# Gate tiles of block 2 in 512-wide products

## The reference

```
h = rms_norm(x, g_attn)
proj = h @ w_in                      # q, k, v of two attentions, and gates: 2 x 1024 columns
o_diff = differential attention, 4 heads
o_sb   = stick-breaking attention, 8 heads
g_diff, g_sb = split(sigmoid(gates + b_gate))
merged = g_diff * (o_diff @ w_o_diff) + g_sb * (o_sb @ w_o_sb)
x = x + merged @ w_out
x = x + (silu(h2 @ w_gate) * (h2 @ w_up)) @ w_down,   h2 = rms_norm(x, g_ffn)
```

## Time and profile before

| | |
|---|---|
| median of three runs | 1475.91 us |
| profiled execution | 1474.18 us, span 1472.4 us |
| busy TensorE, its weight loads, VectorE, ScalarE | 1351.3, 1104.7, 785.6, 593.5 us |
| chain that ended last | TensorE 71%, DMA 22%, VectorE 3% |
| mean granted clock of TensorE | 0.965 of full speed |

### The profile page before, as it was taken

One profiled execution on the slowest core, in us unless ns is written; L12 is line 12 of the kernel. 1 busy time (PEld: TensorE's weight loads), 2 busy tenths in 40 slices (PEclk: granted clock), 3 DMA queues, 4 the chain that ended last, 5 costly groups with the idle time before them and its releaser, 6 DMA issues.

```text
span 1472.4 us, 22657 instructions
## 1 busy us (share of the span) xinstructions
PE 1351.3 (92%) x9775; PEld 1104.7 (75%) x9775; DVE 785.6 (53%) x1168; ACT 593.5 (40%) x811; POOL 14.7 (1%) x32
## 2 busy tenths in 40 slices
PE   8999999997776777767899999999999999999998
PEld 7898998753343334333689999888999999988886
DVE  6656677411111011100678877877567786877753
ACT  5554654210100010101536664655433576455542
POOL 0000000000000000000010000000001000000000
PEclk9999999999899798988999999999999999999999
DMA  9553458899999999999764435656536434566640
GB/s 315 190 177 115 170 202 336 358 426 427 426 426 427 427 427 426 427 427 423 282 192 165 172 132 190 195 172 229 200 115 201 172 121 166 172 200 189 225 172 29
DMA packets 117404, 377.08 MB, mean 256 GB/s; under 512 B 8215, under 2 KB 53623, under 8 KB 104759
## 3 DMA queue, kind: packets, MB, share of 16 engines
q1 hardware_dynamic: 115879, 371.52, 66.0%
q0 software_dynamic: 1424, 4.08, 1.0%
HBM read 372.42 MB, written 1.06 MB: 254 GB/s over the span
## 4 chain that ended last, share of the span: by engine, by line
PE 71%; DMA 22%; DVE 3%; issue 1%; ACT 1%; SPq 1%; POOL 0%; ACTq 0%; DVEq 0%
PE bank L658 21%; PE bank L668 10%; DMA SZ<-in_w_exp_up 8%; DMA ring<-in_w_exp_up 6%; PE bank L670 5%; PE bank L947 5%; PE bank L1321 4%; PE bank L1315 4%; PE bank L1122 3%; PE bank L721 3%; PE bank L691 3%; DMA SZ<-in_w_exp_down 3%; DMA tail_hn<-in_w_exp_up 3%; PE bank L1152 2%; PE bank L1075 2%
## 5 line engine op out<-in xcount | busy, mean ns | idle before, releaser
L1909 DVE TENSOR_TENSOR parts<-ring,parts 128x2048 fp32r<-128x2048 f32 x155 | 351.3, 2288 | 79.0 <-ACT parts L1422 76.2
L1422 ACT ACTIVATE parts<-ring 128x2048 fp32r<-128x2048 f32 x152 | 284.9, 1908 | 95.0 <-PE bank L1321 27.4
L658 PE MATMUL bank<-SKr,parts 128*128 128x256 f32 x1824 | 226.5, 284 | 2.2 <-DVE parts L1909 2.2
L658 PEld LDWEIGHTS bank<-SKr,parts 128*128 128x128 f32 x1824 | 220.8, 192 | 3.9 <-DVE parts L1909 1.9
L668 PE MATMUL bank<-hnr,parts 128*128 128x512 f32 x640 | 222.5, 393 | 0.0
L670 PE MATMUL bank<-hnr,parts 128*128 128x256 f32 x640 | 177.9, 278 | 0.0
L668 PEld LDWEIGHTS bank<-hnr,parts 128*128 128x128 f32 x640 | 119.9, 187 | 27.3
L1122 PE MATMUL bank<-ring,TMP 128*32 128x512 f32 x576 | 85.3, 745 | 49.7 <-DMA ring<-in_w_exp_up 49.7
L2303 DVE COPY KV<-bank 128x256 f32<-128x256 f32 x16 | 6.8, 425 | 222.2 <-PE bank L1102 222.2
L670 PEld LDWEIGHTS bank<-hnr,parts 128*128 128x128 f32 x640 | 120.4, 188 | 0.1
L658 PE MATMUL bank<-hnr,parts 128*128 128x256 f32 x864 | 107.8, 285 | 0.0
(11 more groups left out here) (393 smaller groups left out, 2058.9 us busy)
## 6 DMA issues: line engine op xcount, KB each, us to landing
ring<-in_w_in SPq DMA_DIRECT2D x60, 1024.0 KB, 7.3
ring<-in_w_ffn_in SPq DMA_DIRECT2D x44, 1024.0 KB, 7.1
ring<-in_w_exp_gate SPq DMA_DIRECT2D x18, 2048.0 KB, 39.3
ring<-in_w_exp_up SPq DMA_DIRECT2D x18, 2048.0 KB, 43.9
ring<-in_w_exp_down SPq DMA_DIRECT2D x18, 2048.0 KB, 38.8
ring<-in_w_ffn_out SPq DMA_DIRECT2D x20, 1024.0 KB, 6.6
G<-in_w_exp_gate SPq DMA_DIRECT2D x7, 2048.0 KB, 39.1
SZ<-in_w_exp_up SPq DMA_DIRECT2D x7, 2048.0 KB, 43.9
```

The costliest lines, as they stand in the source:

```text
L658: m = mm(b(name)[:, T * half:T * half + T], part(chunk, ws)[:, k, P * mt:P * mt + P], src[xs][:, k, :], start=k == 0 and i == 0, stop=k == ...
L1422: A(parts[:, 2 * (r % 2), 2048 * i:2048 * i + 2048], ring[:, CHUNK[chunk][0], 2048 * i:2048 * i + 2048], ACT.Copy).then_inc(high_made, 1)
L1909: v.tensor_tensor(parts[:, 2 * (r % 2) + 1, at], ring[:, CHUNK[chunk][0], at], parts[:, 2 * (r % 2), at].bitcast(F32), ALU.subtract).then_ ...
```

## The change

The twelve tiles of the head loop are made by `wide_tile`, each in a bank of its own (ga2a, ga2b and so on: twelve names per layer instead of six). Both parts of the input lie side by side in `SKr`, the low part first, so the lower half of a bank gets Whi xlo + Wlo xhi and the upper half Whi xhi. For each tile ScalarE copies the upper half into the tile's place in `hx`, VectorE adds the lower half to it, and when both tiles of a pair are there VectorE multiplies the pair in place by the normalisation factor. The sigmoids wait for these multiplications by a count. In the head loop ScalarE's copies of turn h-1 stand behind the weights of head h+1, and VectorE's additions where the multiplications stood.

```diff
-            s += [name for name, half in GATE_HALVES[h] if half == 0]
+            s += [f"{name}{'ab'[half]}" for name, half in GATE_HALVES[h]]
...
-                 ("ga0", "ga1"), ("ga1", "ga3"), ("gb0", "gb1"), ("gb1", "gb3"), ("proj_diff", "pa3"),
+                 ("ga0", "ga1"), ("ga1", "ga3b"), ("gb0", "gb1b"), ("gb1", "gb3b"), ("proj_diff", "pa3"),
...
-            def wide_tile(chunk, name, mt):
+            def wide_tile(chunk, name, mt, src=hnr, high=0):
...
-                    mm(b(name)[:, :].rearrange("p (s n) -> p s n", s=2), part(chunk, 0)[:, k, P * mt:P * mt + P], hnr[:, :, k, :],
+                    mm(b(name)[:, :].rearrange("p (s n) -> p s n", s=2), part(chunk, 0)[:, k, P * mt:P * mt + P], src[:, :, k, :],
                        start=k == 0, stop=k == KT - 1, skip_group_check=True)
-                    m = mm(b(name)[:, 0:T], part(chunk, 1)[:, k, P * mt:P * mt + P], hnr[:, 0, k, :],
+                    m = mm(b(name)[:, 0:T], part(chunk, 1)[:, k, P * mt:P * mt + P], src[:, high, k, :],
                            start=False, stop=k == KT - 1, skip_group_check=True)
...
                     for name, half in GATE_HALVES[h]:
                         j = int(name[2])
-                        split_tile(f"{name[:2]}{j // 2}{x}", z_parts, name + x, 2 * (j % 2) + half)
+                        wide_tile(f"{name[:2]}{j // 2}{x}", f"{name}{'ab'[half]}{x}", 2 * (j % 2) + half,
+                                  SKr[:, 0:4096].rearrange("p (s k n) -> p s k n", s=2, k=KT), 1)
...
-                def gate_sigmoid(name, z, row):
-
-                    emptied(act, name)
+                def gate_sigmoid(pairs, z, row):
+
+                    act.wait_ge(gate_scaled, 6 * l + pairs)
...
+                def gate_lows_of(h):
+
+                    for name, half in GATE_HALVES[h]:
+                        full(act, f"{name}{'ab'[half]}{x}")
+                        A((ga if name[1] == "a" else gb)[:, 2 * int(name[2]) + half, :], b(f"{name}{'ab'[half]}{x}")[:, T:2 * T],
+                          ACT.Copy).then_inc(gate_low_out, 1)
+
                 for h in range(8):
...
                     if h < 7:
                         sb_weights(h + 1)
+                    if h:
+                        gate_lows_of(h - 1)
                     if h in (0, 2, 4):
                         sb_softplus(h + 2)
...
                 act.preload_act_table(ACT.Sigmoid)
-                gate_sigmoid("ga3" + x, ga, 0)
+                gate_lows_of(7)
+                gate_sigmoid(2, ga, 0)
                 second_highs("bo3" + x, 3)
                 high("proj_sb" + x)
-                gate_sigmoid("gb3" + x, gb, 8)
+                gate_sigmoid(6, gb, 8)
...
                     for name, half in GATE_HALVES[h]:
+                        z, j, bank = ga if name[1] == "a" else gb, int(name[2]), f"{name}{'ab'[half]}{x}"
+                        dve.wait_ge(gate_low_out, 12 * l + sum(len(g) for g in GATE_HALVES[:h]) + GATE_HALVES[h].index((name, half)) + 1)
+                        freed(v.tensor_tensor(z[:, 2 * j + half, :], b(bank)[:, 0:T], z[:, 2 * j + half, :], ALU.add), bank)
                         if half:
-                            take_scaled(name + x, two(ga if name[1] == "a" else gb, int(name[2])), by_attn)
+                            emptied(dve, f"{name}a{x}")
+                            emptied(dve, bank)
+                            v.tensor_tensor(two(z, j), two(z, j), by_attn, ALU.mult).then_inc(gate_scaled, 1)
```

More of the change, by code:

```diff
@@ L377, in build @@
         hid_silu, hid_scaled = sem("hid_silu"), sem("hid_scaled")
+        gate_low_out, gate_scaled = sem("gate_low_out"), sem("gate_scaled")
         low_sum_out, gate_rooted = sem("low_sum_out"), sem("gate_rooted")
```

## The result

The changed kernel's median is 1476.57 us over 22 runs (1474.36 to 1479.18), that of the kernel before 1474.11 us over 22 (1471.58 to 1476.58): ratio 1.0014, 95% interval 1.0008 to 1.002, so 2.1 us more, between 1.2 and 2.9 (the two medians are 2.46 apart). I had forecast +2.4 us, and 1478.3 as the median; the measured one is 1.7 lower because the kernel before, at 1475.91 over three runs, came to 1474.11 over 22. In a second job the ratio was 1.0013 (1.0004 to 1.0021). The profiled execution has a span of 1474.9 us.

The account below looks back on a forecast made before the run. TensorE's time was taken as the bound, VectorE a close second. Per layer -1.25 + 0.47 + 1.86 + 0.11 = +1.19 us, both layers +2.4; forecast 1478.3 us, range 1473.4 to 1480.8.

Parts of the forecast that it names:

- TensorE's saving: Head loop's twelve gate tiles: the wide form saves 0.104 us a tile, 1.25 us per layer, 2.50 us in both.
- The walk of VectorE's order: Head loop from 823.21: gate additions wait for ScalarE's copies, so head 6's stick pieces start at 845.19 instead of 841.91.
- rival 1: VectorE's gate blocks lose 0.08 us of overlap 11 times, 0.9 us per layer; +4.2 us, 1480.1; chance 0.25.
- The standstills: TensorE waits for VectorE's stick pieces before L1255: 0.47 us at head 4, 1.86 us at head 6, per layer.
- the restart: TensorE's first L1255 pair after a standstill takes 0.70 us instead of 0.59, 0.11 us more per layer.
- The sum: Per layer -1.25 + 0.47 + 1.86 + 0.11 = +1.19 us; both layers +2.4 us.
- What I cost at nothing: ScalarE's later queue (0.6 us spare), VectorE's last subtractions before the merge (0.7 spare), banks and DMAs: no added time.
- The banks: Six more names per layer; tightest reuse is head 5's score bank, wanted about 825.2, freed at 825.05; others 0.7 us or more.
- The second: Rival: VectorE has hidden slack in the head loop and TensorE never waits; -2.5 us, 1473.4; chance 0.13.
- The third: Rival: TensorE's 1.9 us standstill also lowers its clock, twice 1.6 us more; 1481.5; chance 0.04.
- The fourth: Rival: TensorE saves 2.5 ns a pair, not 13; four tiles behind head 6 give 0.08 us, not 0.42; 1479.0; chance 0.03.

Follow-up runs that it names:

- e3: Changed kernel with ScalarE's copies of turn h-1 ahead of head h+1's exponential instead of behind it; ratio to before 0.9979, head loop 47.26 us.
- e1: Changed kernel with each head-loop gate tile made by three 256-wide products per input tile again; ratio to before 1.0025, head loop 49.99 us.
- e2: Changed kernel with VectorE's gate additions and multiplications moved behind the mask and stick pieces of the same turn; ratio to before 1.001, head loop 48.89 us.
- e7: Kernel of e3 with 0.9 us of unused VectorE work in turn 4, between gate additions and mask; one run, head loop 47.62 us.
- e5: Changed kernel with 0.9 us of unused VectorE multiplications in turn 4, ahead of head 6's stick pieces; one run, head loops 52.13 and 50.67 us.
- c2: Changed kernel, unchanged, run again in a second job; ratio to before 1.0013, head loop 49.77 us.
- e6: Changed kernel with 0.9 us of unused VectorE multiplications in turn 5, behind head 6's stick pieces; one run, head loop 49.79 us.

## Why the prediction was right

**TensorE's saving** was over-sized. I took 346.7 ns a pair and 0.104 us a tile from the feed-forward stage. TensorE's timeline of the changed kernel, two neighbouring 512-wide products in turn 0 and two in turn 2:

```profile
814.16 0.39 PE L669 MATMUL bank<-SKr,parts 128*128 128x512 f32 x1
...
814.51 0.39 PE L669 MATMUL bank<-SKr,parts 128*128 128x512 f32 x1
```

```profile
828.21 0.40 PE L669 MATMUL bank<-SKr,parts 128*128 128x512 f32 x1
...
828.56 0.40 PE L669 MATMUL bank<-SKr,parts 128*128 128x512 f32 x1
```

In turn 0 the mean over 14 pairs is 347.1 ns, as I said; in the other turns it is 353 ns, and the tile costs 2.82 us instead of 2.773. Two tiles at 0.10 and ten at 0.05 give 0.71 us per layer instead of 1.25. e3 has two more tiles at the faster pace, and its head loop measures 0.80. The Trainium skill ("VectorE: DVE Perf Modes", the section on the trn2 errata) prices a matmul at its columns plus 6 cycles. By it an estimate of the saving is 0.24 us per layer; the measurement lies between that and my rows, about halfway.

**The walk of VectorE's order** held turn by turn, within 0.25 us. I had the additions at 828.57 and 842.02 and head 6's pieces at 845.19; they came at 828.69, 842.22 and 845.50, of which 0.06 is a later start of the whole stretch. What is left, 0.06, 0.14 and 0.25 us, grows from turn to turn. Hand-overs and copies were as the rows of before had them, and rival 1's loss of overlap did not happen: the additions (0.76 for two) and the mask still start 0.34 apart.

**The standstills** were forecast at 0.47 and 1.86 us and 0.11 for the restart, 2.44 in all. The loop's growth (1.74) plus the saving (0.71) is 2.45. The trace calls 0.35 and 1.62 idle, since it counts from the modelled end of the last product. That the sum agrees so well is in part luck. VectorE's pieces for head 6 came 0.25 us later than in the walk and the step from VectorE to TensorE takes 0.14 us and not 0.04; but TensorE too came later to its wait, since the eight tiles ahead of it saved 0.50 us and not 0.83. The price of the restart was misread: I took the products at 838.59 as standing behind a gap, but TensorE was never idle there. Behind the standstills the first pair takes 0.67 against 0.60 in the earlier trace rows, 0.07 more and not 0.11.

**The sum.** Head loops: 2 x 1.74 = +3.5 us, against +2.4 forecast. As VectorE alone sets when head 6's sums start (e1), the smaller saving of the tiles ahead of them costs nothing. They start 1.86 us later than before and not 1.50 (846.82 against 845.32), which is the walk (0.25) and the hand-over (0.10). Behind them the loop wins 0.12 us back and not 0.31, since the four tiles there save 0.21 and not 0.42. Together that is 0.55 us per layer, 1.1 in all. The total came to +2.1 because 0.9 to 1.05 us came back between the layers, which no step of mine contained. That the forecast's number is so near is luck: two errors of opposite sign, about 1 us each. Its mechanism is right by itself.

**What I cost at nothing** was free. ScalarE's split of out0 after the merge still waited for TensorE, 0.61 us where I had 0.6 to spare; the first output's low parts ended at 861.61, 0.66 before the merge, where I had 0.7. ScalarE's row answers to the earlier trace rows:

```profile
874.14 3.72 ACT L1424 ACTIVATE parts<-ring 128x2048 fp32r<-128x2048 f32 x2 [0.61 <-PE bank L948]
```

The banks held in the changed kernel; e2 shows how near the edge they are. **The rivals:** the first (lost overlap, +4.2 us) did not occur, though the walk was 0.25 us short per layer. The second (VectorE has slack, -2.5 us) became true only in e3, and with 1.6 us from the head loops. The third (clock) did not occur at 1.6 us, but see below. The fourth (TensorE saves less) was half true: behind head 6's sums the tiles saved half of what I had said, where the rival said a fifth.

## What to carry to other kernels

When work for a helper engine goes behind a hand-shake, look at which side of it the instruction stands: the same copies cost 2.5 us per layer behind ScalarE's exponential and nothing ahead of it, because VectorE waited in order for both. A walk through one engine's in-order queue with durations from the trace finds such a standstill; here its steps added up to 0.25 us too little over five turns. The price of a product form should be taken from the place where it will run, if the trace has anything like it; 2% on a tile was two fifths of the gain that I had counted on.

## What the runs showed of the hardware

- The same pair of products (512 and 256 wide) runs at one of two rhythms, 347 or 353 ns in the mean over a tile, for whole tiles at a time. In the changed kernel turn 0 has the first and all others the second, in both layers and both profiles; in e3 the tiles gb0b and gb2a have the first as well (347.5), in e7 gb0b alone. In e7 gb2a, which follows a standstill of 0.08 us, is at 353; in layer 1 of e5, behind one of 2.53 us, it is at 347. So what happens ahead of a tile can change it, but not in one direction. The cause stays open; no run tried it.
- A standstill of TensorE of 2.54 us in e5 was followed by a lower granted clock in layer 0 and one of 2.53 us was not in layer 1; the six of 1.62 us in the changed kernel, c2 and e6 never were. The windows of e5, length, busy TensorE, clock, DMA, in layer 0 and layer 1:

```profile
849.60:855.90 6.30, 6.21 (x30) 0.73 0.18 73
...
1226.10:1230.80 4.70, 4.65 (x31) 1.00 0.23 92
```

  From head 6's to head 7's key sums it took 6.24 us in layer 0 and 4.63 in layer 1: 1.6 us for the clock, as the third rival priced it from the earlier trace rows. At the merge the two layers are 1.46 apart.
